# Weight rounding and splitting around the first units of MLPs and gated units, the root copied by VectorE, and an input freed chunk by chunk

## The reference

```python
# first stack, layer i, after the attention
y = square(relu(rmsnorm(x, g[2]) @ w1[i])) @ w2[i]        # w1: 1024 x 4096
x = x + rmsnorm(y, g[3])
x = x + sigmoid(x @ ple_gate_w[i]) * (p[i] @ ple_w[i])    # embedding gate
# second stack, twice a layer
gu = rms_norm(h, ln) @ w13                                # w13: 1024 x 5632
h = h + 0.5 * ((silu(gu[:, :2816]) * gu[:, 2816:]) @ w2)
# rmsnorm(x, g) = x * rsqrt(mean(x * x) + eps) * g
```

## Time and profile before

| | us |
|---|---|
| median of 3 runs | 3194.69 |
| lowest and highest | 3194.19, 3195.99 |
| profiled execution, its span | 3194.1 |
| TensorE busy | 3025.0 (95%) |
| VectorE busy | 2114.5 (66%) |
| ScalarE busy | 1534.9 (48%) |
| mean granted TensorE clock | 0.966 of full |

### The profile page before, as it was taken

How to read it: one execution, slowest core, us unless ns; L and a number is a source line. 1 busy time by engine, 2 the same in 40 slices (tenths; PEclk the granted TensorE clock), 3 DMA queues, 4 the chain that set the end, 5 groups by cost and what they waited for, 6 DMA issues and landing times.

```text
span 3194.1 us, 44762 instructions
## 1 busy us (share of the span) xinstructions
PE 3025.0 (95%) x18902; PEld 2701.3 (85%) x18902; DVE 2114.5 (66%) x2561; ACT 1534.9 (48%) x2075; POOL 28.5 (1%) x22
## 2 busy tenths in 40 slices
PE   8899998899999999899899999999999999999999
PEld 7878896788997889788888978989888888898987
DVE  4567666576646765576587686637778768664676
ACT  5543455444644445534444654544444465454443
POOL 0000000000000000000000000000000000000000
PEclk9999988999999999899999999999999989999999
DMA  6345541255434553255365433525556543353463
GB/s 218 111 145 190 172 159 54 80 185 187 147 119 146 185 182 125 93 187 199 128 206 175 144 123 132 145 93 185 188 168 200 173 143 125 120 166 97 146 201 102
DMA packets 381731, 482.53 MB, mean 151 GB/s; under 512 B 32988, under 2 KB 330155, under 8 KB 381532
## 3 DMA queue, kind: packets, MB, share of 16 engines
q1 hardware_dynamic: 380684, 476.50, 46.1%
q0 software_dynamic: 560, 2.13, 0.2%
q10 hardware_dynamic: 288, 1.05, 0.1%
HBM read 478.53 MB, written 1.08 MB: 150 GB/s over the span
## 4 chain that ended last, share of the span: by engine, by line
PE 80%; DVE 12%; ACT 5%; issue 3%; DMA 0%; DVEq 0%; ACTq 0%; SPq 0%
PE ps L401 16%; PE ps L402 16%; PE ps L403 16%; PE ps L428 14%; PE ps L429 7%; DVE wl L384 4%; ACT wh L374 3%; PE ps L427 2%; DVE ar L2331 1%; PE ps L426 1%; PE ps L499 1%; PE ps L1284 1%; DVE ar L1224 1%; DVE sm L1229 1%; PE ps L2480 1%
## 5 line engine op out<-in xcount | busy, mean ns | idle before, releaser
L384 DVE TENSOR_TENSOR wl<-raw,wh 128x2048 fp32r<-128x2048 f32 x456 | 1037.6, 2281 | 517.1 <-ACT wh L374 516.9
L374 ACT ACTIVATE wh<-raw 128x2048 fp32r<-128x2048 f32 x456 | 863.8, 1901 | 458.8 <-PE ps L403 239.0
L428 PE MATMUL ps<-ahl,wh 128*128 128x512 f32 x1904 | 683.3, 398 | 0.0
L401 PE MATMUL ps<-ahl,wh 128*128 128x256 f32 x1928 | 573.2, 297 | 31.2 <-DVE ahl L576 13.7
L402 PE MATMUL ps<-ahl,wh 128*128 128x256 f32 x1928 | 562.8, 292 | 0.0
L403 PE MATMUL ps<-ahl,wl 128*128 128x256 f32 x1928 | 562.0, 292 | 0.0
L429 PE MATMUL ps<-ahl,wl 128*128 128x256 f32 x1904 | 534.0, 280 | 0.0
L401 PEld LDWEIGHTS ps<-ahl,wh 128*128 128x128 f32 x1928 | 388.5, 202 | 42.1 <-issue 30.6
L428 PEld LDWEIGHTS ps<-ahl,wh 128*128 128x128 f32 x1904 | 358.2, 188 | 77.1
L401 PE MATMUL ps<-wh,ar_r 128*128 128x512 f32 (+1 forms) x944 | 370.0, 392 | 23.9 <-issue 17.8
L402 PEld LDWEIGHTS ps<-ahl,wh 128*128 128x128 f32 x1928 | 388.8, 202 | 0.3 <-issue 0.2
(11 more groups left out here) (403 smaller groups left out, 4109.3 us busy)
## 6 DMA issues: line engine op xcount, KB each, us to landing
raw<-in_ffn_w SPq DMA_DIRECT2D x264, 512.0 KB, 4.5
raw<-in_mlp_w SPq DMA_DIRECT2D x256, 512.0 KB, 4.4
raw<-in_w_in SPq DMA_DIRECT2D x124, 512.0 KB, 4.5
raw<-in_da_w_in SPq DMA_DIRECT2D x48, 512.0 KB, 4.8
raw<-in_ple_gate_w SPq DMA_DIRECT2D x32, 512.0 KB, 4.5
raw<-in_w_ssd_out SPq DMA_DIRECT2D x32, 512.0 KB, 4.1
raw<-in_fox_w_in SPq DMA_DIRECT2D x24, 512.0 KB, 4.7
raw<-in_nsa_w_in SPq DMA_DIRECT2D x20, 512.0 KB, 4.9
```

Of the source, the lines that this page charges most:

```text
L374: nc.scalar.activation(wh[:, slot, 0:sizes[n]], raw[:, slot, 0:sizes[n]], ACT.Copy).then_inc(s_hi, E.adds(s_hi))
L384: nc.vector.tensor_tensor(wl[:, slot, 0:sizes[n]], raw[:, slot, 0:sizes[n]], wh[:, slot, 0:sizes[n]].bitcast(F32), ALU.subtract).then_inc( ...
L401: nc.tensor.matmul(o, wa, xa, start=start, stop=False)
L428: nc.tensor.matmul(o, wa, both, start=start, stop=False)
```

## The change

It touches the start of each of the four MLPs, the start of each of the four gated units, and the embedding gate of the fourth layer.

- MLP and gated unit, ScalarE: one `act_hi` moves ahead of the square root, and the next directly behind it. The copy of the spread root goes.
- VectorE: after the reciprocal comes a `dve_lo`, then the copy of the spread root from PSUM, with a wait for its own end. In the MLP both first ReLUs follow; the `dve_lo` that stood between ReLU and square of unit 0 is the one now ahead of the copy, and that of unit 1 now stands behind the low part of unit 0. In the gated unit, of the two `dve_lo` in the middle of unit 0 one is ahead of the copy and one behind the low part.
- TensorE: the spread comes after four of the eight chunks of the first half of `pe_wide`, not after all eight.
- Last embedding gate: the fourth block goes chunk by chunk through both halves (`pe_freeing`), and each chunk raises `s_fr`. ScalarE overwrites chunks 0 to 3 of `ahl` ahead of the last tanh, 4 to 7 behind it. VectorE does `add(2)` and two `dve_lo` ahead of the scaled chunks.

SyncE's and GpSimd's rows stay in their order. The wait counts were adjusted (`E.skip`), in `dve_ssd` too.

```diff
+        def pe_freeing(E, b0, s):
+            n, a, b = pe_block(E, S, DC)
+            for k in range(DC):
+                for m in range(2):
+                    c = slice(m * P, (m + 1) * P)
+                    last = mm3(bank(b0)[:, m, :], a[:, k, c], b[:, k, c], ah[:, k], al[:, k], k == 0 and m == 0, k == DC - 1 and m == 1)
+                if k < DC - 1:
+                    last.then_inc(s_fr, E.adds(s_fr))
+            ends(E, n, last, s)
...
         def pe_wide(E, b0, s, between=None):
...
                     last = mm2(ps[:, b0 + m, :], a[:, k, c], b[:, k, c], k, k == 0, k == DC - 1)
+                    if between is not None and m == 0 and k == 3:
+                        between()
                 if m:
                     ends(E, n, last, s)
-                elif between is not None:
-                    between()
...
-        def act_spread(E, b):
+        def dve_spread(E, b):
             E.eng.wait_ge(s_rs, E.next(s_rs))
-            nc.scalar.activation(st[:, :], ps[:, b, 0:S], ACT.Copy).then_inc(s_st, E.adds(s_st))
+            nc.vector.tensor_copy(st[:, :], ps[:, b, 0:S]).then_inc(s_st, E.adds(s_st))
+            E.eng.wait_ge(s_st, E.sofar(s_st))
...
-        def act_scaled(E, gcol, squares=True, his=()):
-            for c in range(DC):
+        def act_scaled(E, gcol, squares=True, his=(), chunks=range(DC), freed=False):
+            for c in chunks:
+                if freed:
+                    E.eng.wait_ge(s_fr, E.next(s_fr))
...
         def act_mlp(E):
+            act_hi(E)
             act_std(E, DC, 7)
-            act_spread(E, 7)
             act_hi(E)
-            act_hi(E)
+            E.skip(s_rs)
...
         def dve_mlp(E):
             dve_rstd(E)
-            E.eng.wait_ge(s_st, E.next(s_st))
-            for u in range(N_MLP):
-                if u < 2:
-                    E.eng.wait_ge(s_md, E.next(s_md))
-                else:
-                    dve_halves(E, 2 - 2 * (u % 2), rr[:, u % 2])
+            dve_lo(E)
+            dve_spread(E, 7)
+            def relu(u):
                 nc.vector.scalar_tensor_tensor(out=rr[:, u % 2], in0=bank(u) if u < 2 else rr[:, u % 2], scalar=0.0, in1=st[:, :].unsqueeze(1).to_broadcast([P, 2, S]),
                                                op0=ALU.max, op1=ALU.mult).then_inc(s_hr, E.adds(s_hr))
-                if u == 0:
-                    dve_lo(E)
-                if u == 1:
-                    dve_lo(E)
+            for u in range(2):
+                E.eng.wait_ge(s_md, E.next(s_md))
+                relu(u)
+            for u in range(N_MLP):
                 if u >= 2:
+                    dve_halves(E, 2 - 2 * (u % 2), rr[:, u % 2])
+                    relu(u)
                     dve_lo(E)
...
-                if u >= 2 and u < N_MLP - 1:
+                if u == 0 or 2 <= u < N_MLP - 1:
                     dve_lo(E)
...
         def pe_ple(E, normed):
...
-            pe_T(E, ah, al, 7, s_mm)
             if normed:
+                pe_T(E, ah, al, 7, s_mm)
...
+            else:
+                pe_freeing(E, 7, s_mm)
...
         def act_ple(E, normed, gcol=None):
...
+                act_hi(E)
+                act_scaled(E, gcol, chunks=range(0, 4), freed=True)
+                gate(3)
+                act_scaled(E, gcol, chunks=range(4, DC - 1), freed=True)
+                act_scaled(E, gcol, chunks=range(DC - 1, DC))
+                act_hi(E)
...
         def dve_ple(E, gcol=None):
...
-                if gcol is not None and j:
-                    dve_scaled(E, gcol, 2 * j - 2)
-                    dve_scaled(E, gcol, 2 * j - 1)
             add(0)
             add(1)
             dve_lo(E)
...
+            else:
+                add(2)
+                dve_lo(E)
+                for c in range(4):
+                    dve_scaled(E, gcol, c)
+                add(3)
+                for c in range(4, DC):
+                    dve_scaled(E, gcol, c)
+                dve_lo(E)
                 dve_lo(E)
...
         def act_glu(E):
+            act_hi(E)
             act_std(E, DC, 7)
-            act_spread(E, 7)
+            act_hi(E)
+            E.skip(s_rs)
             for u in range(N_GLU):
-                act_hi(E)
-                if u == 0:
+                if u:
                     act_hi(E)
...
         def dve_glu(E):
             dve_rstd(E)
-            E.eng.wait_ge(s_st, E.next(s_st))
+            dve_lo(E)
+            dve_spread(E, 7)
...
                     nc.vector.tensor_tensor(v, bank(1), rstd, ALU.mult).then_inc(s_hr, E.adds(s_hr))
+                else:
                     dve_lo(E)
-                dve_lo(E)
...
-                if u:
-                    dve_lo(E)
+                dve_lo(E)
```

More of the change, by code:

```diff
@@ L261, in build @@
         s_tri = sem("s_tri")
+        s_fr = sem("s_fr")
         scratch = nc.dram_tensor("bias_rows", [H64, 512], F32, kind="Internal").ap()
@@ L851, in pe_ple, with act_ple @@
                 pe_spread(E, 3, s_rb)
-        def act_ple(E, normed):
+            else:
+                pe_freeing(E, 7, s_mm)
+        def act_ple(E, normed, gcol=None):
             act_hi(E)
@@ L871, in act_ple @@
             gate(2)
-            act_hi(E)
-            square(2)
-            gate(3)
-            square(3)
+            if normed:
+                act_hi(E)
+                square(2)
+                gate(3)
+                square(3)
+            else:
+                act_hi(E)
+                act_scaled(E, gcol, chunks=range(0, 4), freed=True)
+                gate(3)
+                act_scaled(E, gcol, chunks=range(4, DC - 1), freed=True)
+                act_scaled(E, gcol, chunks=range(DC - 1, DC))
+                act_hi(E)
         def dve_ple(E, gcol=None):
@@ L894, in dve_ple @@
             dve_lo(E)
-            dve_lo(E)
-            add(2)
-            dve_lo(E)
[L898 to L901, removed]
+            if gcol is None:
+                dve_lo(E)
[3 more added lines that the diff above has]
+            else:
+                add(2)
+                dve_lo(E)
+                for c in range(4):
+                    dve_scaled(E, gcol, c)
+                add(3)
+                for c in range(4, DC):
+                    dve_scaled(E, gcol, c)
+                dve_lo(E)
                 dve_lo(E)
@@ L3003, in _ @@
                 act_rows_post(E, None, False, 0)
-                act_ple(E, layer + 1 < DEPTH)
-            act_scaled(E, gg("ln_ffn1_2", 0, 8))
-            act_hi(E)
+                act_ple(E, layer + 1 < DEPTH, gg("ln_ffn1_2", 0, 8))
             for layer in range(DEPTH2):
```

## The result

| | before | changed |
|---|---|---|
| median of 4 runs, us | 3194.44 | 3161.52 |
| lowest and highest | 3193.5, 3195.99 | 3155.71, 3167.11 |
| ratio, with its 95% interval | | 0.9888 (0.9877 to 0.9900) |

What follows compares the result with a forecast made beforehand. The prediction took TensorE's stalls at MLP, gated unit and last gate, and the half clock after them, to bound the kernel. Savings of 12.8 + 7.9 + 3.4 + 9.9 = 34.0 us gave 3160.7 us, range 3155 to 3172.

Steps and rivals of the forecast that it cites:

- MLP, stall: Four MLP starts: TensorE's wait at the first down product falls from 3.3 to 0.1 us each, saving 12.8 us.
- MLP, clock: Four MLPs: without the stalls, 16.96 us of TensorE work at half clock runs at full clock, saving 7.9 us.
- Gated units: Four gated unit starts: stalls of 1.15 us go, smaller waits come at the spread; net 3.4 us, bounds 0 to 4.6.
- new wait at the spread: Gated unit starts: TensorE waits 0.1 to 0.3 us at the spread, since the root comes later.
- Rival (b): Gated units: a table switch costs more than its row, turning the gain into a 1.7 us loss; 3165.8 us, chance 0.05.
- Last gate: End of last embedding gate: 7.5 us of stall goes and the next pair takes 11.6 instead of 14.00; 9.9 us.
- GpSimd's interference: Last gate: GpSimd's adds slow VectorE's splits and chunks by 1 us; at twice that, the start is 1.5 late.
- Rival (c): Last gate stays late through ScalarE's chunk waits and GpSimd's adds; half of the 9.9 us stays, 3165.6 us, chance 0.05.
- (a): MLPs and last gate: the clock is not given back, 7.9 + 2.4 us stay; 3171.0 us, chance 0.12.
- (e): MLP starts: rounding gets its slot only after the sums, root 1.9 us later, 5 us of stalls; 3166 us, chance 0.05.
- (d): Later units: denser work lowers the clock elsewhere; 90 us of new half clock would give 3202.6 us, chance 0.03.
- margin of 4 us for the clock: Whole kernel: 4 us added below the forecast's bounds for half-clock stretches elsewhere that may change length.

Runs made afterwards that it cites:

- mlp_only: The kernel before with the MLP part of the change alone, against the kernel before (3198.25 us): median 3177.69 us, ratio 0.9937 (0.9924 to 0.9949).

## Why the prediction was right

- **Sum.** 34.0 us forecast, 32.9 measured beside the kernel before and 35.5 when both were measured again.
- **MLP, stall**: 3.3 to 0.1 us each was forecast, and no stall is left. The chain came as worked out: the rounding ahead of the root in time, the copy in 0.41 us (0.45 taken).
- **MLP, clock**: 7.9 us. `mlp_only` gained 20.6 against the 20.7 of stall and clock together. But half clock behind such a stall is no certainty; the four of the profiled execution, 20.5 us at half or 5.1 each, lie above the 4.3 us each of the twelve starts. Scaled by that, the term is some 6.6 us instead of 7.9, an estimate. One profiled execution was the only scale, and that it came this near the mean was luck.
- **Gated units**: 3.4 forecast, 3.4 measured, but the measured interval reaches from 0.6 to 6 us, so it is luck that the two agree to a tenth. The trace gives 4.6 - 0.7 = 3.9. The new wait at the spread was put at 0.1 to 0.3 and is 0.17; the root was said to come 0.9 us later (0.8 in the working) and comes 0.83 later. The drain that the Trainium skill ("ScalarE: Activation LUTs", "What ACT_TABLE_LOAD costs") adds to a load shows in no row: the load starts 0.02 us behind the end of the rounding (2162.87 + 1.91), and the root 0.02 us behind the end of the load (2164.80 + 1.28). Rival (b) falls.
- **Last gate**: 9.9 forecast; the trace shows 7.52 + 14.00 - 11.52 = 10.0. The low part was ready ahead of TensorE's end, as said. GpSimd's interference was bounded well and fell where nobody waited. Rival (c) falls.
- **Rivals** (a) and (e) fall with the clock of 1.00 behind the MLP starts and with the root in its place; (d) falls because the denser MLPs hold the clock: from each of the four MLP roots on it is 1.00 for about 200 us, in both traces of the changed kernel.
- **What the prediction gave too much weight**: the copy's change of engine and the early spread. Each was counted as a link of the stall; taken back alone, one costs nothing and the other 0.6 us per MLP. The split behind both ReLUs costs 1.23 us. These pieces do not add up to 3.30 us, since each hides part of another, and the rounding's share is only estimated (1.6 us). And its range for the gated units reached to no gain, while the run-to-run spread, 11 us, was wider than its margin of 4 us for the clock.

## What to carry to other kernels

When the fastest engine stalls at a stage's start, list what the helpers do in program order between the event it waits for and the event before, and move what is not needed for it (here preparing later weights) into the time when they idle anyway, ahead of the dependency; check that its own inputs are free by then. Count with a stall what the clock costs after it: here a stall of 2 us cost an estimated 1.6 us more, one of 1.2 us nothing. Where several edits are made at one place, take each back alone: some of them may carry little or nothing.

## What was not expected of the hardware

The clock's answer to a stall is not a fixed price. With nearly the same program around it, at the first down product of an MLP, none of the stalls of 0.62 and 1.23 us (four each) was followed by half clock, all four of 2.04 us were by 3.4 us of it, and of twelve stalls of 3.30 us two were followed by none, five by 3.4 and five by 6.8 us. Four 128x256 operations of VectorE took 2.71 us instead of 1.66 where GpSimd was adding in the same time.
